# Delta-net scan: the key–state products moved between the dependent levels, and the subtraction from the values moved behind the level-32 copies

## What is computed

```python
lmat = jnp.where(strict, jnp.einsum('bhncd,bhnsd->bhncs', kb, k) * decay, 0.0)
tmat = lax.linalg.triangular_solve(eye + lmat, jnp.broadcast_to(eye, lmat.shape), left_side=True, lower=True)
u_w = tmat @ (v * beta[..., None])
w_w = tmat @ (kb * jnp.exp(gc)[..., None])
...
def step(s, inp):
    qd, kd, uu, ww, aa, gl = inp
    v_new = uu - ww @ s
    o = qd @ s + aa @ v_new
    s = s * jnp.exp(gl)[..., None, None] + jnp.einsum('bhcd,bhce->bhde', kd, v_new)
    return s, o
```

## Time and profile before

| | |
|---|---|
| median of three runs | 2936.38 us (2935.12 to 2938.29) |
| profiled execution, its own time | 2935.71 us |
| span of the profiled execution | 2933.9 us |
| the eight rounds of the scan | from 980.90 to 1171.36 us of the span |
| PE busy over the span | 2659.6 us (91%) |
| DVE, ACT, POOL busy | 1194.7, 784.7, 1626.8 us |

### The profile page before, as it was taken

One profiled execution on the slowest core, in us unless ns is written; L12 is line 12 of the kernel. 1 busy time (PEld: TensorE's weight loads), 2 busy tenths in 40 slices (PEclk: granted clock), 3 DMA queues, 4 the chain that ended last, 5 costly groups with the idle time before them and its releaser, 6 DMA issues. The chain is left out here.

```text
span 2933.9 us, 45691 instructions
## 1 busy us (share of the span) xinstructions
PE 2659.6 (91%) x16477; PEld 2136.4 (73%) x16477; DVE 1194.7 (41%) x2212; ACT 784.7 (27%) x1482; POOL 1626.8 (55%) x1665
## 2 busy tenths in 40 slices
PE   6988999999998898899999899778999998878986
PEld 4756677786787788667778578667677786767886
DVE  2463322223479666432232301665322223453455
ACT  2252322211532333132211330331322112252311
POOL 3402666665566122566667555664666675708985
PEclk9999999999999789999999899999999998999998
DMA  6333455422222000355532122002555332203442
GB/s 233 115 127 117 144 172 172 143 101 72 74 73 86 1 2 1 102 172 172 172 113 100 61 86 72 1 1 73 172 172 172 129 100 72 87 1 101 163 152 86
DMA packets 217161, 305.60 MB, mean 104 GB/s; under 512 B 7331, under 2 KB 155550, under 8 KB 217023
## 3 DMA queue, kind: packets, MB, share of 16 engines
q1 hardware_dynamic: 179007, 228.16, 23.5%
q10 hardware_dynamic: 38016, 75.50, 7.9%
HBM read 302.60 MB, written 1.05 MB: 103 GB/s over the span
## 5 line engine op out<-in xcount | busy, mean ns | idle before, releaser
L582 POOL TENSOR_TENSOR w_lo<-w_raw,w_hi 128x512 fp32r<-128x512 f32 x720 | 948.0, 1317 | 108.1 <-POOL w_hi L579 88.1
L579 POOL TENSOR_SCALAR w_hi<-w_raw 128x512 fp32r<-128x512 f32 x720 | 472.1, 656 | 872.9 <-PE bank L1038 607.6
L1038 PE MATMUL bank<-u_lo,w_hi 128*128 128x512 f32 (+1 forms) x2144 | 809.8, 378 | 43.9 <-DVE u_lo L1697 22.4
L1038 PE MATMUL bank<-u_hi,w_lo 128*128 128x512 f32 (+1 forms) x2144 | 791.7, 369 | 0.0
L1038 PE MATMUL bank<-u_hi,w_hi 128*128 128x512 f32 (+1 forms) x2144 | 791.3, 369 | 0.0
L1038 PEld LDWEIGHTS bank<-u_lo,w_hi 128*128 128x128 f32 x2144 | 408.8, 191 | 182.2 <-issue 99.1
L1038 PEld LDWEIGHTS bank<-u_hi,w_hi 128*128 128x128 f32 x2144 | 408.9, 191 | 68.3
L1038 PEld LDWEIGHTS bank<-u_hi,w_lo 128*128 128x128 f32 x2144 | 409.4, 191 | 62.8
L1605 PE MATMUL bank<-gs_lo,w_hi 128*128 128x512 f32 (+1 forms) x576 | 212.1, 368 | 10.1 <-DVE gs_lo L2298 6.7
L1605 PE MATMUL bank<-gs_hi,w_lo 128*128 128x512 f32 (+1 forms) x576 | 210.9, 366 | 0.0
L1605 PE MATMUL bank<-gs_hi,w_hi 128*128 128x512 f32 (+1 forms) x576 | 210.8, 366 | 0.0
(11 more groups left out here) (333 smaller groups left out, 3867.2 us busy)
## 6 DMA issues: line engine op xcount, KB each, us to landing
w_raw<-in_ffn_w_up SPq DMA_DIRECT2D x88, 1024.0 KB, 7.1
ada_w<-in_ada_w ACTq DMA_DIRECT2D x72, 1024.0 KB, 5.2
w_raw<-in_ffn_w_down SPq DMA_DIRECT2D x44, 1024.0 KB, 4.9
ada_w<-in_ada_w SPq DMA_DIRECT2D x16, 1024.0 KB, 5.1
w_raw<-in_gdn_w_in SPq DMA_DIRECT2D x16, 1024.0 KB, 5.7
w_raw<-in_attn_w_qkv SPq DMA_DIRECT2D x12, 1024.0 KB, 5.2
w_raw<-in_gla_w_in SPq DMA_DIRECT2D x12, 1024.0 KB, 5.3
ada<-in_ada_w SPq DMA_DIRECT2D x8, 1024.0 KB, 13.9
```

The costliest lines, as they stand in the source:

```text
L579: eng.tensor_scalar(w_hi[:, q, :], src, 1.0, 0.0, ALU.mult, ALU.add).then_inc(pool.own, pool.step())
L582: eng.tensor_tensor(w_lo[:, q, :], src, w_hi[:, q, :].bitcast(F32), ALU.subtract).then_inc(w_split, 1)
L1038: mm = eng.matmul(bank[banks[m]][:, T], w[:, q, c:c + P], v[:, k, T], start=(k == 0 and n == 0), stop=(k == KT - 1 and n == 2))
```

## The change

On PE the eight matmuls of keys by state no longer stand together behind L1353. They are in a function `key_state(d)`: direction 0 is called behind L1372 (the first product of level 32), direction 1 behind L1386 (the second). On DVE the subtraction L2033 moves behind the four groups of copies of level 32. No instruction is added, removed or changed in size.

```diff
@@ PE
-                        if first:
-                            eng.wait_ge(st_upd, pe.next(st_upd))
-                        for d in range(2):
+                        def key_state(d):
+
+                            if first and d == 0:
+                                eng.wait_ge(st_upd, pe.next(st_upd))
                             if not first:
                                 eng.wait_ge(bo_ready, pe.next(bo_ready))
                             for b in range(4):
                                 mm = eng.matmul(bank[6 + d][:, C(b)], bk[:, H(b), tok[d]], bS[:, d, H(b), :], start=True, stop=True)
                             mm.then_inc(ks_ready, 1)
+
...
                             mm.then_inc(a_ready, 1)
+                        key_state(0)
                         for d in range(2):
                             TTm, Am = bt[d][4:6]
                             eng.wait_ge(diag_ready, pe.next(diag_ready))
...
                             mm.then_inc(b_ready, 1)
+                        key_state(1)
                         for d in range(2):
                             NLm = bt[d][3]
@@ DVE
+                        for d in range(2):
+                            TTm = bt[d][4]
+                            eng.wait_ge(b_ready, dve.next(b_ready))
+                            i, o = slice(96 * d, 96 * d + 32), slice(32 + 32 * d, 64 + 32 * d)
+                            eng.tensor_copy(bT[o, :, i], quad(bank[3 * d + 1][o, :])[:, :, i])
+                            for q in range(2):
+                                i, o = slice(64 * q + 32 * d, 64 * q + 32 * d + 32), slice(64 * q + 32 - 32 * d, 64 * q + 64 - 32 * d)
+                                ins = eng.tensor_copy(TTm[i, :, o], quad(bank[3 * d + 2][i, :])[:, :, o])
+                            ins.then_inc(t_ready, 1)
                         for d in range(2):
                             Dm = bt[d][0]
                             eng.wait_ge(ks_ready, dve.next(ks_ready))
...
                             ins.then_inc(y_ready, 1)
-                        for d in range(2):
-                            TTm = bt[d][4]
...
-                            ins.then_inc(t_ready, 1)
```

## The result

The changed kernel's median is 2912.4 us (2907.77 to 2915.93, six runs), that of the kernel before on the same chips 2938.95 us (2935.12 to 2940.93, six runs): a ratio of 0.9911, with a 95% interval of 0.9899 to 0.9922. It is faster, by 26.5 us at the medians. The predicted time was 2912.6.

A forecast was written before the change was run, and what follows sets the result against it. PE was taken to bound the scan, so reordering could win only its idle time and clock: 2935.7 − 9.8 (order) − 14.0 (clock) = 2911.9, or 2912.6 as median; range 2908 to 2927.

The forecast's parts named there:

- What is late ahead of L1399: Level 32 of a scan round: DVE's queue ends last, its subtraction L2033 standing before the copies PE waits for.
- The term of order: Scan rounds: DVE's copies start 1.22 us earlier, 9.8 us over 8 rounds (8.0 to 11.2).
- the changeover between 128x128 and 32x32 matmuls: On PE, around the moved key–state products: each switch of matmul size taken as 0.09 us.
- The wait for `bNL`: PE, direction 1 of L1372: a 0.26 us wait for DVE appears that the moved products used to cover.
- my own sign: Changed profile: order term is wrong if L1385 starts later than 2.2 us behind L1374.
- the bounds that I gave for DVE's start: DVE's level-32 copies: start taken 0.5 us behind L1382's product, bounds said to give 1.0 to 1.4 us earlier.
- The cover for the subtraction: DVE ahead of L2049: the moved subtraction ends at 1161.53, the copy is wanted at 1161.77, so 0.24 us spare.
- Rival 3: DVE reaches L2049 late and L1414 with it; each us beyond 0.24 costs a us per round; chance 0.08.
- The clock's term: Scan: PE's clock no longer falls to 0.50 behind the small matmuls, held in all eight rounds; 14.0 us.
- rival 2: Scan: clock falls as before, only the gain from order remains; 2925.9, or 2926.6 on the median's scale; chance 0.13.
- rival 4: Scan, L1372 to L1414: clock stays low for longer, making the kernel slower, about 2953; chance 0.04.
- the longest piece without a dense matmul: PE, end of direction 1's products to L1399: 1.2 us, like 1.28 us in the last round where the clock held.

The follow-up runs named there:

- the longer subtraction: Changed kernel with each of DVE's subtractions split into two halves of 64 columns, same results; 2918.47 us, ratio 0.9941 to the kernel before.
- The dense filling: Kernel before, with two extra unread 128x128 matmuls (4 records) in each of PE's waits ahead of L1382 and L1394; 2923.67 us, ratio 0.9942.
- the small filling: Kernel before, with 16 records of unread 32x32 matmuls in each of PE's waits ahead of L1382 and L1394; 2939.04 us, ratio 0.9996.

## Why the prediction was right

**What is late ahead of L1399.** Right: DVE's queue was the later one, but only by 0.27 us, as the run with DVE's half shows. What makes the remaining 0.8 us of a round is that PE reaches the second product of level 32 earlier. The run with direction 0 left in front puts this on direction 1's products alone: 21.55 with DVE's half, 20.75 with direction 1 also moved, 20.73 with both.

**The term of order**, 1.22 us a round: at full clock 21.82 became 20.72, so **1.10**, 8.8 us over eight rounds against 9.8. The mis-sized piece is the changeover between 128x128 and 32x32 matmuls. I took 0.09 us for each; L1385 starts 1.09 us behind the first of direction 0's products, where 8 records at 0.112 are 0.90, so 0.19 for that changeover. L1385 is then at 7.77 us of the round (predicted 7.65) and DVE's copy 0.50 later, exactly the value that I took. The wait for `bNL` (predicted 0.26 us) shows inside L1374, 1.29 us long instead of 0.85; 0.21 of it is seen as a wait of the weight loads. L1403 is at 10.62 against 10.50, and from there to the end the round has the 10.10 us of the earlier trace rows. Two flaws of the working did no harm. By my own sign the order term counts as wrong: L1385 starts 2.31 us behind L1374 (1052.21 less 1049.90), and I had named 2.2 as the limit; that was the very value that I predicted (1157.19 less 1154.99), so the sign left no room for an error of 0.1. And the bounds that I gave for DVE's start, 0.4 to 0.87 us behind L1382, make the term 0.85 to 1.32 us a round and not 1.0 to 1.4; 1.10 lies in both.

**The cover for the subtraction**, 0.24: a wait of 0.20 in the profile and 0.30 by the longer subtraction. Rival 3 did not happen, and it is shown that it could have.

**The clock's term**, 14.0 us: the fall is gone in all rounds. The dense filling, which gives 13.95 us with PE's own order untouched, shows that the term is separate from the order's and was sized rightly. The sum 8.8 + 13.95 is the scan's 22.6 within 0.2. By the rule of the Trainium skill's page "TensorE: Matmul & The Clock Gate" (The HAM clock gate), as I read it in rival 2, the time would have been near 2926. It was not, and the small filling, beside the run with direction 0 in front, speaks against idleness as what drops the clock here.

One argument against rival 4 was misread: I wrote that in the old order the clock came back as soon as L1414's dense matmuls ran. So it was in the third round, where 0.50 ended at 1046.05 and L1414 began at 1046.27. In the second L1414 began at 1022.03 and 0.50 lasted until 1025.57, 3.5 us into dense work. The rival did not happen, but it was less unlikely than I made it.

**What was less sure than it looked.** I argued from the longest piece without a dense matmul, 1.2 us. The last round before had already held its clock behind 4.48 us without one, so holding behind a short piece once proved little. The kernel with direction 0's products in front has such a piece of 2.3 us (L1375 at 1047.95 to direction 1's products at 1050.26) and its clock holds. The one with both behind has one of 2.4 in a round that holds (L1374 at 1072.81 to 1075.22) and the same 2.4 in one that falls (1008.74 to 1011.14, the clock down from about 1012.0, within the products). The length of the piece alone does not tell these rounds apart, and I cannot say from these runs how far the changed kernel is from a fall. That it holds is shown; the rule by which it holds is open.

**The agreement of the total** is partly luck. The medians differ by 26.5 us where I had summed 23.8, and the profiled scans differ by 22.6; the reference for my sum, the median shown with the kernel before, was 2.6 us below the one measured later.

## What to carry to other kernels

Where the granted clock of a stretch is below 1, price the fall as a term of its own, by comparing rounds of the same work at the two levels, before costing any change of order; here it was the larger term, and a matmul of no use to anyone won it. Moving dense matmuls from a dense stretch into a thin one can gain twice, by filling waits and by the clock. But when a producer is moved back in one queue, look at what waits for it in the other and at what stands behind that: PE's half of this change alone made the kernel 15 us slower, because a queue in program order waited for what had been moved back, while DVE's half alone gained 10.6 us.

## What the runs showed of the hardware that I had not expected

- The clock's answer to added dense work was not in proportion. Four dense records in one wait, or in the other, left 2938.4 and 2935.99 us (beside 2939.36 and 2936.34 before); in both, 2923.67 (beside 2939.11). One half made single falls longer (a round of 25.54 us, against 24.10 at most before, its first round aside).
- 32x32 matmuls in the waits left the clock falling with PE idle for 0.62 us of the thin stretch, where a stretch with eight records of 128x128 held it with 0.64 us idle.
- Between a group of 128x128 matmuls and a following group of 32x32 matmuls lay 0.19 us at L1385 in the changed kernel, and 0.09 at L1372 before, with no wait recorded at either.
